# Prompt attention head by head and value pages in column strips, threaded through the gate units of a hybrid decoder step

## The chip, the cores and the metric
The kernel runs on one core of a Trainium2 chip. The metric is the device time of one launch in microseconds (us), the median of several runs. A profiled execution has a time of its own, and its span runs from the first to the last instruction on the core. Engines: TensorE (PE, with its weight loads listed as PEld), VectorE (DVE), ScalarE (ACT), GpSimd (POOL), SyncE (SP). Each works off its own queue in order and waits on semaphores.

## The reference, cut to what matters
One layer for a prompt of 256 tokens and 8 samples of one token each (together 264 columns), all float32, width 2048:

```python
h = rms_norm(x, norm1_w);  z = h @ w_in        # conv B,C,X | q,k,v | memory q | 3 gates of 2048
y_conv = (zb * short_conv(zc * zx)) @ w_conv_out
o  = (softmax(q1 k1^T) - lam * softmax(q2 k2^T)) V    # 8 heads, head width 64 + 64, values 128
y_diff = (rms_norm(o, subln_w) * (1 - lam_init)) @ w_diff_out
y_mem  = softmax(qm mk^T) mv @ w_cross_out            # 4 heads of 256 over 256 memory tokens
merged = g0 * y_conv + g1 * y_diff + g2 * y_mem       # g = sigmoid of the gate part of z
x = x + merged @ w_o;  x = x + peer_ffn(rms_norm(x))  # product-key experts, top 16 of 8 heads
```

For the prompt, keys, values and memory come from this step. Each sample has 16 pages of 128 cached keys and values, found through a page table, and 256 cached memory tokens.

## The kernel before, in words
Every engine has its own program, written out by hand in the order in which the work is to run; there is no planner. The stages follow each other on PE:

- Lines 541 to 598: norms, transposes and the projections for q, k, v, memory q and the convolution, while DVE and POOL work through the samples' key pages.
- Lines 625 to 635: keys and values of the prompt's memory; the convolution's state; own scores of the samples.
- Lines 637 to 670: a gate unit (`gate_chunk`) is 16 matmuls of 128x264 into bank 0 or 1 (one gate chunk), then 8 matmuls into bank 2 (one branch chunk). ACT takes the sigmoid, DVE multiplies and adds (a merge). There are 48 units: 16 for the convolution branch, 16 for memory, 16 for differential attention. Before the gate matmuls a unit waits for the sigmoid two units back (`gate_done`), before the branch matmuls for the merge of the unit ahead of it (`y_taken`). The first 8 units (`PART`) carry small steps of the samples' softmax at given places.
- Lines 680 to 726: prompt attention as a stage of its own, two heads at a time in two halves of PSUM. ACT copies queries, keys and values to a work area, PE turns them, ACT copies them out, PE makes the scores, DVE adds the mask and takes maxima, ACT the exponentials, DVE normalises, PE turns the weights back, ACT copies, PE multiplies with the values, ACT copies the outputs.
- Lines 734 to 780: units 8 to 15, each with one sample's values. Two memory pages and ten value pages are multiplied on PE with the weights of 4 or 8 heads as the stationary operand (line 752: two matmuls of 512 columns a page), six pages are weighed and summed on DVE (`weigh_page`) and go through PE as one more. The sums for all heads by all columns are masked to each head's own columns on DVE (`mask_sums`) and turned to a column by eight small matmuls (`columns`, line 761). POOL fetches pages into a ring of 4 slots for PE and 2 for DVE (line 459).
- Lines 782 to 800: units 16 to 47, with the sums of the sub-norm after unit 23.
- From line 802: output projection, router projection, and the expert stage, which gathers rows of two large tables.

SP streams the weights of gates and branches through a ring of two blocks (lines 284 to 320); a block serves two units. The memory key norm on DVE (line 1400) comes between the merges of units 4 and 5.

Of the kernel before, what the change touches and what calls it, by code (L numbers as in the profile page):

```python
# [19 lines left out]
ds = bass.ds  # L20
# [55 lines left out]
def build(nc, A, O):  # L76
# [16 lines left out]
    with ctx:  # L93
# [3 lines left out]
        def sem(name):  # L97
# [24 lines left out]
        PART = 8  # L122
        temp = [ring4[:, :, :].rearrange("p a b -> p (a b)"), bregion[:, :]]
# [12 lines left out]
        mask = work[:, 0:2 * TP].rearrange("p (t n) -> p t n", t=2)  # L136
        sg = work[:, 1024:1024 + 2 * NT].rearrange("p (s n) -> p s n", s=2)
# [35 lines left out]
        weighed = work[:, 0:DC]  # L173

        own_heads = [sq_mkv[0:n, o:o + DC] for n, o in ((MH, 2 * DC), (HEADS, 3 * DC))]
# [16 lines left out]
        a_now = [zst[:, n, 0:PAGES * HEADS].rearrange("p (t h) -> p t h", t=PAGES) for n in range(2)]  # L192
        am_now = [zst[:, n, PAGES * HEADS:PAGES * HEADS + 2 * MH].rearrange("p (t h) -> p t h", t=2) for n in range(2)]
        Ad_f, Sm_f = cs_rows, Sm[:, :, :, :].rearrange("p a b c -> p (a b c)")
        tmpm = small[:, 0:3, :].rearrange("p a b -> p (a b)")[:, 0:NT]
# [5 lines left out]
            exp_in exp_out sum_in sum_full a_ready attn_staged tt_full qk_T s_full sm_ready exp_ready  # L201
# [5 lines left out]
            n2_in lam_pre lam_exp x1_rows n2_ss sums_free weights_staged dpage_used weighed_ready  # L207
            weighed_used sums_masked columns_done sub_taken gather_turn loop_turn""".split()
# [4 lines left out]
        v_landed = [sem(f"v_landed{i}") for i in range(VR + DR)]  # L213
# [39 lines left out]
        selfA = small[:, 4, 64:128].rearrange("p (h b) -> p h b", h=HEADS)  # L253

# [4 lines left out]
        def _(sp):  # L259
# [32 lines left out]
            for b in range(3):  # L292
                if b == 0:
                    for r in range(NR):
                        sp.wait_ge(s["chunk_full"], C_O - 2 * (NR - 1 - r))
                        fetch(r, w_in, gate_col[b] + r * BLK)

                    sp.wait_ge(s["chunk_full"], C_O)
                    for r in range(NR):
                        branch_weights(b, r, r)  # L300
                    for n in (2, 3):
                        gate_weights(b, n, n % NR)
                        branch_weights(b, n, n % NR)
                    for n in (4, 5):
                        gate_weights(b, n, n % NR)

                    sp.wait_ge(s["attn_done"], 2)
                    for n in (4, 5):
                        branch_weights(b, n, n % NR)
                    for n in (6, 7):  # L310
                        gate_weights(b, n, n % NR)
                        branch_weights(b, n, n % NR)
                else:
                    for r in range(NR):
                        gate_weights(b, r, r)
                        branch_weights(b, r, r)
                    with sp.Fori(0, 8 // NR - 1) as i:
                        for r in range(NR):
                            gate_weights(b, NR + r, r, i)
                            branch_weights(b, NR + r, r, i)  # L320
# [14 lines left out]
        def _(pool):  # L335
# [3 lines left out]
            pool.sem_inc(s["vpage_used"], VR)  # L339
            pool.sem_inc(s["dpage_used"], DR)  # L340
# [88 lines left out]

            pool.wait_ge(s["a_ready"], 1)  # L430
            st(nc.gpsimd.memset(mask[:, :, :], 0.0))
# [4 lines left out]
            pool.wait_ge(s["mk_ready"], 1)  # L436
            for c, name in ((0, "mem_k_prompt"), (1, "mem_v_prompt")):
                pool.dma_start(O[name][0, 0].rearrange("(t p) h d -> p t (h d)", p=P),
                               mkv[:, :, c * DC:(c + 1) * DC]).then_inc(s["mkv_stored"], 16)


            pool.wait_ge(s["attn_done"], 2)
            pool.wait_ge(s["qk_stored"], 64)
            with pool.Fori(0, TS) as b:
                for k in range(DP):

                    for n in (2 * k, 2 * k + 1, PV + k):
                        if n < PV:
                            pool.wait_ge(s["vpage_used"], b * PV + (n + 1))
                            r = n % VR  # L450
                        else:
                            pool.wait_ge(s["dpage_used"], b * DP + (k + 1))
                            r = VR + k % DR
                        if n < 2:
                            src = cmem_v[ds(b * NM + n * P, P), :]
                        else:
                            page = pool.value_load(pt[0:1, ds(b * PAGES + (n - 2), 1)], min_val=0, max_val=POOL_PAGES - 1)
                            src = cache_v[ds(page * PAGE, PAGE), :]
                        pool.dma_start(v_slots[r], src).then_inc(v_landed[r], 16)  # L459


            pool.wait_ge(s["vpage_used"], TS * PV + VR)
            pool.wait_ge(s["dpage_used"], TS * DP + DR)
            pool.dma_start(x_rows[:, 0:2, :], A["x_prompt"][0].rearrange("(t p) d -> p t d", p=P)).then_inc(s["x_again"], 16)
            pool.dma_start(x_rows[0:TS, 2, :], A["x_sample"].rearrange("b t d -> (b t) d")).then_inc(s["x_again"], 16)
# [69 lines left out]
        def _(pe):  # L535
# [64 lines left out]
            def conv_state():  # L600
                pe.wait_ge(s["conv_ready"], 1)
                pe.wait_ge(s["rows_taken"], 32 + 2)
                for j in range(BC):
                    last = nc.tensor.transpose(ps[0:2 + TS, 4 + j // 4, (j % 4) * P:(j % 4 + 1) * P], conv[:, BC + j, TP - 2:NT], ident[:, :])
                last.then_inc(s["cs_full"], 1)

            def own_scores():

                pe.wait_ge(s["self_in"], 1)
                mm(ps[:, 7, 0:P], ones[0:TS, :], small[0:TS, 0, :], start=True, stop=True).then_inc(s["self_full"], 1)  # L610

            def turn_maxima(m, n):
                pe.wait_ge(s["max_full"], m + 1)
                nc.tensor.transpose(ps[0:n, 5, 0:P], small[:, 1, 0:n], ident[:, :]).then_inc(s["max_diag"], 1)

            def spread_maxima(m, n):
                pe.wait_ge(s["mb_full"], m + 1)
                mm(ps[:, 6, 0:n], ones[0:n, :], small[0:n, 2, 0:n], start=True, stop=True).then_inc(s["max_diag"], 1)

            def sum_partitions(m, n):  # L620
                pe.wait_ge(s["sum_in"], m + 1)
                mm(ps[:, 7, 0:n], ones[:, :], small[:, 1, 0:n], start=True, stop=True).then_inc(s["sum_full"], 1)
# [10 lines left out]
            conv_state()  # L633
            own_scores()
            pe.wait_ge(s["chunk_taken"], C_O + 4)

            def gate_chunk(b, r, c, q, operand, between=None, ready=None):

                pe.wait_ge(s["gate_done"], q + 1)
                for k in range(KC):  # L640
# [3 lines left out]
                    if between:  # L644
                        between(k)
# [4 lines left out]
                for k in range(BC):  # L650
# [3 lines left out]
                    if between:  # L654
                        between(KC + k)
# [3 lines left out]
            after = {(0, KC - 1): (turn_maxima, 0, nk), (0, KC + BC - 1): (spread_maxima, 0, nk), (1, KC + BC - 1): (sum_partitions, 0, nk),  # L659
                     (2, KC + BC - 1): (turn_maxima, 1, nm), (3, KC - 1): (spread_maxima, 1, nm), (4, KC - 1): (sum_partitions, 1, nm)}  # L660
            for q in range(PART):
                g, r, c = q // 2, q // 2 % NR, q % 2
# [3 lines left out]

                def softmax_step(k):
                    if (q, k) in after:
                        after[q, k][0](*after[q, k][1:])
                gate_chunk(0, r, c, q, conv[:, 0:BC, :], softmax_step)  # L670
            pe.wait_ge(s["a_ready"], 1)
            pe.wait_ge(s["gate_done"], PART + 2)
            pe.wait_ge(s["y_taken"], PART + 2)


            def flat(u):
                b = 4 - 4 * u
                return ps[:, b:b + 4, :].rearrange("p a b -> p (a b)")

            def attention(n_heads, base, w):  # L680
                halves = w // P
                a0 = 1536
                s0 = 512 * halves
                with pe.Fori(0, n_heads // 2) as i:
                    for u in range(2):
                        pe.wait_ge(s["attn_staged"], i * 2 + (base + u + 1))
                        for o in range(2):
                            for f in range(halves):
                                for t in range(2):
                                    last = nc.tensor.transpose(  # L690
                                        flat(u)[:, (o * halves + f) * 256 + t * P:(o * halves + f) * 256 + (t + 1) * P],
                                        temp[u][:, (2 * o + t) * w + f * P:(2 * o + t) * w + (f + 1) * P], ident[:, :])
                        last.then_inc(s["tt_full"], 1)
                    for u in range(2):
# [1093 lines left out]
```

## Time and profile before
| what | value |
|---|---|
| median of 3 runs (lowest, highest) | 3098.11 us (3096.09, 3110.02) |
| the profiled execution, its span | 3102.36 us, 3100.2 us |
| mean granted clock of TensorE in it | 0.945 |
| busy: PE, DVE, ACT, POOL | 2669.5, 1488.6, 370.3, 1047.9 us |

A busy time says how long an engine had an instruction in work, not that it was at its peak; ends of matmuls are modelled, so two neighbours can overlap in the records by a short tail. The granted clock is a share of 2.4 GHz. A float32 matmul shows as two instructions, each with its weight load.

### The profile page before, as it was taken

The numbers are of one execution on the slowest core, as the hardware profiler recorded it, in microseconds if no ns is written. First come the engines' busy times: TensorE is split into PE (matmuls) and PEld (weight loads), VectorE is DVE, ScalarE is ACT, GpSimd is POOL, SyncE is SP. The second block draws the span as 40 slices with busy tenths as digits, with TensorE's granted clock in tenths as the row PEclk, the third lists the DMA queues.
The fourth block names the chain that finished last, engine by engine and source line by source line (L and its number), as shares of the span: only waits on it lengthen the run. The fifth ranks groups of instructions, "written<-read, shape, count | busy, mean of one in ns | idle before, by whom it ended". The sixth has DMA issues, their size and how long they took to land.

```text
span 3100.2 us, 29862 instructions
## 1 busy us (share of the span) xinstructions
PE 2669.5 (86%) x9145; PEld 1635.6 (53%) x9145; DVE 1488.6 (48%) x2527; ACT 370.3 (12%) x816; POOL 1047.9 (34%) x952
## 2 busy tenths in 40 slices
PE   6899999895699999999999968777789959777777
PEld 4678888774433336888887743333233314233333
DVE  1456567733233331120002768887655455555543
ACT  3111000013400000100002111101111101111110
POOL 1256562200022220000000555556644545555532
PEclk9899999997799999999998989999989979999999
DMA  5599996931177875353443999999999999999999
GB/s 159 182 314 329 324 334 235 329 121 68 36 248 267 269 260 192 125 174 126 135 135 109 355 359 419 421 417 413 413 421 419 416 365 422 418 421 416 415 421 380
DMA packets 305386, 913.54 MB, mean 295 GB/s; under 512 B 15634, under 2 KB 195946, under 8 KB 236652
## 3 DMA queue, kind: packets, MB, share of 16 engines
q0 software_dynamic: 122304, 723.48, 58.8%
q1 hardware_dynamic: 182980, 188.92, 18.8%
q8 instruction: 38, 0.62, 0.1%
q14 instruction: 64, 0.52, 0.0%
HBM read 905.80 MB, written 6.56 MB: 294 GB/s over the span
## 4 chain that ended last, share of the span: by engine, by line
PE 58%; DMA 21%; DVE 10%; issue 5%; POOL 5%; ACT 1%; ACTq 0%; DVEq 0%; POOLq 0%; SPq 0%
PE ps L564 19%; PE ps L641 11%; DMA sb_S<-in_peer_u_dram,sb_ring 8%; PE ps L844 6%; PE ps L752 6%; PE ps L651 6%; DMA sb_bregion<-in_peer_u_dram,sb_ring 5%; PE ps L631 3%; DVE sb_bregion L1688 2%; DVE sb_S L1688 1%; POOL sb_bregion L478 1%; DMA sb_S<-in_peer_v_dram,sb_ring 1%; DMA sb_wring<-in_peer_v_dram,sb_ring 1%; DMA sb_wring<-in_w_in_dram 1%; DMA sb_mkv<-in_peer_u_dram,sb_ring 1%
## 5 line engine op out<-in xcount | busy, mean ns | idle before, releaser
L844 PE MATMUL ps<-sb_wring,sb_ring 128*128 128x512 f32 x992 | 468.8, 624 | 132.6 <-DMA sb_wring<-in_peer_v_dram,sb_ring 80.4
L564 PE MATMUL ps<-sb_hT,sb_wring 128*128 128x264 f32 x2304 | 534.7, 394 | 16.0 <-DMA sb_wring<-in_w_peer_q_dram 7.1
L564 PEld LDWEIGHTS ps<-sb_hT,sb_wring 128*128 128x128 f32 x2304 | 443.5, 194 | 99.3 <-issue 19.8
L844 PEld LDWEIGHTS ps<-sb_wring,sb_ring 128*128 128x128 f32 x992 | 191.2, 199 | 411.4 <-issue 282.0
L1688 DVE CUSTOM_DVE_ANT_0 sb_bregion<-sb_bregion,sb_rows 128x2048 f32<-128x2048 f32 x128 | 293.8, 2295 | 228.7 <-DMA sb_bregion<-in_peer_u_dram,sb_ring 221.0
L641 PE MATMUL ps<-sb_hT,sb_wring 128*128 128x264 f32 x1536 | 375.3, 396 | 18.5 <-DMA sb_bregion<-in_w_conv_out_dram 18.5
L641 PEld LDWEIGHTS ps<-sb_hT,sb_wring 128*128 128x128 f32 x1536 | 288.1, 192 | 122.1 <-issue 76.3
L478 POOL DMA_INDIRECT sb_bregion<-in_peer_u_dram,sb_ring x132 | 192.0, 1454 | 271.3 <-DVEq L1140 210.3
L844 PE MATMUL ps<-sb_hT,sb_ring 128*128 128x512 f32 x496 | 232.4, 618 | 44.4 <-DMA sb_hT<-in_peer_v_dram,sb_ring 34.3
L844 PE MATMUL ps<-sb_oreg,sb_ring 128*128 128x512 f32 x496 | 226.0, 603 | 39.9 <-DMA sb_oreg<-in_peer_v_dram,sb_ring 34.6
L1107 ACT ACTIVATE sb_ring<-sb_ident,sb_ring 128x128 f32<-128x128 f32 x248 | 99.7, 402 | 913.8 <-PE ps L844 705.4
L1688 DVE CUSTOM_DVE_ANT_0 sb_S<-sb_S,sb_rows 128x2048 f32<-128x2048 f32 x64 | 146.7, 2293 | 109.4 <-DMA sb_S<-in_peer_u_dram,sb_ring 105.6
L1688 DVE CUSTOM_DVE_ANT_0 sb_mkv<-sb_mkv,sb_rows 128x2048 f32<-128x2048 f32 x64 | 146.7, 2293 | 106.2 <-DMA sb_mkv<-in_peer_u_dram,sb_ring 103.2
L478 POOL DMA_INDIRECT sb_wring<-in_peer_v_dram,sb_ring x128 | 160.7, 1255 | 95.0 <-PE ps L844 53.6
L844 PEld LDWEIGHTS ps<-sb_hT,sb_ring 128*128 128x128 f32 x496 | 95.0, 197 | 179.9 <-issue 138.6
L752 PE MATMUL ps<-sb_rows,sb_zst 128*8 128x512 f32 (+1 forms) x384 | 185.7, 607 | 1.8 <-DMA sb_rows<-in_cache_mem_v_dram 1.8
L844 PEld LDWEIGHTS ps<-sb_oreg,sb_ring 128*128 128x128 f32 x496 | 92.4, 192 | 170.2 <-issue 144.3
L1517 DVE SCALAR_TENSOR_TENSOR sb_S<-sb_rows,sb_zst,sb_S 128x128 f32<-128x128 f32 x320 | 87.6, 347 | 155.0 <-DMA sb_rows<-in_cache_v_dram 154.7
L1551 DVE TENSOR_TENSOR sb_small<-sb_S,ps 128x264 f32<-128x264 f32 x32 | 13.7, 429 | 289.5 <-PE ps L651 289.2
L459 POOL DMA_DIRECT2D sb_rows<-in_cache_v_dram x128 | 68.0, 531 | 235.3 <-issue 231.3
L478 POOL DMA_INDIRECT sb_mkv<-in_peer_u_dram,sb_ring x66 | 102.5, 1553 | 128.3 <-DVEq L1140 105.3
L510 POOL COPY sb_ring<-sb_ring 128x16 int32<-128x16 int32 x16 | 18.3, 1141 | 371.4 <-DVEq L1140 371.4
(349 smaller groups left out, 2861.8 us busy)
## 6 DMA issues: line engine op xcount, KB each, us to landing
sb_wring<-in_w_in_dram SPq DMA_DIRECT2D x52, 2048.0 KB, 11.4
sb_rows<-in_cache_v_dram POOLq DMA_DIRECT2D x128, 512.0 KB, 4.8
sb_ring<-in_cache_k_dram POOLq DMA_DIRECT2D x64, 512.0 KB, 6.6
sb_mkv<-in_cache_k_dram POOLq DMA_DIRECT2D x64, 512.0 KB, 6.1
sb_wring<-in_w_mem_kv_dram SPq DMA_DIRECT2D x8, 2048.0 KB, 8.7
sb_wring<-in_w_o_dram SPq DMA_DIRECT2D x8, 2048.0 KB, 8.1
sb_wring<-in_w_peer_q_dram SPq DMA_DIRECT2D x8, 2048.0 KB, 12.4
sb_ring<-in_cache_mem_k_dram POOLq DMA_DIRECT2D x16, 512.0 KB, 6.8
```

Source lines behind the costliest of these rows:

```text
L459: pool.dma_start(v_slots[r], src).then_inc(v_landed[r], 16)
L478: nc.gpsimd.indirect_dma_start(dst, None, table, bass.IndirectOffsetOnAxis(ap=idx, axis=0)).then_inc(landed, 16)
L510: st(nc.gpsimd.tensor_copy(uidx[:, g % 4, :], idx_flat[:, g * TOPK:(g + 1) * TOPK]))
L564: last = mm(ps[:, (2 * r + c) % 4, 0:NT], wring[:, r, k, c * P:(c + 1) * P], rhs[:, k, :], start=(k == 0), stop=(k == KC - 1))
L631: last = mm(ps[:, 2 * r + t, 0:BLK], memT[:, k, t * P:(t + 1) * P], wring[:, r, k, :], start=(k == 0), stop=(k == KC - 1))
L641: last = mm(ps[:, c, 0:NT], wring[:, r, k, c * P:(c + 1) * P], hT[:, k, :], start=(k == 0), stop=(k == KC - 1))
L651: last = mm(ps[:, 2, 0:NT], bwring[:, r, k, c * P:(c + 1) * P], operand[:, k, :], start=(k == 0), stop=(k == BC - 1))
L752: last = mm(ps[0:w.shape[1], bank + q, :], w, block[:, q * 512:(q + 1) * 512], start=first, stop=final)
L844: last = mm(ps[:, 4 * t + q, :], diag[:, k % 4, :], e_slots[v % ER][:, q * 512:(q + 1) * 512], start=False, stop=q_stop, skip_group_check= ...
L1107: st(A_(diag[:, k % 4, :], ident[:, :], ACT.Copy, scale=wexp[:, g % 4, j:j + 1]))
L1517: st.run(STT(weighed[:, at], page, w, weighed[:, at], ALU.mult, ALU.add))
L1688: st(V.tensor_tensor_reduce(out=u_slots[n % UR], in0=u_slots[n % UR], in1=h2, scale=1.0, scalar=0.0, op0=ALU.mult, op1=ALU.add, accum_out= ...
```

## The change
It does five things.

1. Prompt attention is no longer a stage. Its 12 heads (now the 4 memory heads first, then the 8 differential ones) run one at a time, head a in units 2a+1 and 2a+2. PE's steps sit at fixed matmuls of a unit: turning at 0 and scores at 8 of the odd unit, turning back at 6 and values at 14 of the even one (`aside`). Queries, keys and values are read where they lie, without staging; one work area and banks 3 to 5 serve all heads.
2. The samples' values go through PE entirely, no page through DVE. A round takes four pages, each into its own 32 output partitions of banks 6 and 7 (`value_round`). Four rounds hold the memory pages of all samples (units 7 to 10), 32 rounds the value pages (units 11 to 26, two a unit), four rounds a sample. Masking and columns follow per sample, or per two samples for memory: 12 times in all.
3. Pages go to 11 slots, in places that are free by then; POOL issues them in one fixed order.
4. Units 0 to 31 are written out; a merge of the later branches signals behind its second step. The sub-norm's steps sit in units 28 to 31.
5. The memory key norm is done right behind the page maxima, ahead of the samples' memory scores; ACT takes its root between memory chunks 10 and 11. The prompt's memory stores come earlier on POOL, and the state's transposes use banks 6 and 7.

```diff
@@ slots @@
-        VR, DR = 4, 2
-        v_slots = [rows[:, t, c * DC:(c + 1) * DC] for t in range(2) for c in range(3)]
-        DP = 6
-        PV = 2 + PAGES - DP
+        late_slots = [sq_mkv[:, n * DC:(n + 1) * DC] for n in range(4)]
+        early_slots = [rows[:, 2, n * DC:(n + 1) * DC] for n in (0, 1, 3, 2)] + [ring_flat[:, D + DC:2 * D], work[:, 0:DC], work[:, DC:2 * DC]]
+        v_slots = late_slots + early_slots
+        MEM_PAGES, VPAGES = 2 * TS, (2 + PAGES) * TS
+        MEM_ROUNDS = MEM_PAGES // 4
+        QUAD = 32
@@ POOL @@
+            def load_page(p):
+                slot = page_slot(p)
+                earlier = [e for e in range(p) if page_slot(e) == slot]
+                if earlier:
+                    pool.wait_ge(s["vpage_used"], earlier[-1] + 1)
...
+                pool.dma_start(v_slots[slot], src).then_inc(v_landed[slot], 16)
@@ PE @@
+            def value_round(n):
+                pages = range(4 * n, 4 * n + 4)
+                if n == 0:
+                    pe.wait_ge(s["a_ready"], 1)
+                elif n < MEM_ROUNDS:
+                    pe.wait_ge(s["sums_masked"], n)
+                elif n % 4 == 0:
+                    pe.wait_ge(s["sums_masked"], MEM_ROUNDS + (n - MEM_ROUNDS) // 4)
+                for p in pages:
+                    pe.wait_ge(v_landed[page_slot(p)], 16 * (page_use(p) + 1))
+                for q in range(2):
+                    for p in pages:
+                        g = p % 4
...
+                        last = mm(ps[g * QUAD:g * QUAD + w.shape[1], 6 + q, :], w, v_slots[page_slot(p)][:, q * 512:(q + 1) * 512], start=first, stop=final)
+                        if q == 1:
+                            last.then_inc(s["vpage_used"], 1)
+            def aside(q, k):
...
+                a = (q - 1) // 2
+                if 0 <= a < ATTN:
+                    if (q % 2, k) == (1, 0):
+                        turn_in(a)
+                    if (q % 2, k) == (1, 8):
+                        scores_of(a)
+                    if (q % 2, k) == (0, 6):
+                        turn_back(a)
+                    if (q % 2, k) == (0, 14):
+                        outputs_of(a)
+                if 7 <= q < 11 and k == 18:
+                    value_round(q - 7)
+                if 8 <= q < 12 and k == 10:
+                    columns(q, q - 8)
+                if 11 <= q < 27 and k in (6, 18):
+                    value_round(MEM_ROUNDS + 2 * (q - 11) + k // 18)
+                if 13 <= q < 29 and q % 2 and k == 12:
+                    columns(q, MEM_ROUNDS + (q - 13) // 2)
...
+            for q in range(32):
...
+                if q == 6:
+                    pe.wait_ge(s["columns_kept"], 1)
+                if 9 <= q < 13:
+                    pe.wait_ge(s["columns_kept"], q - 7)
+                if 14 <= q < 30 and q % 2 == 0:
+                    pe.wait_ge(s["columns_kept"], 1 + MEM_ROUNDS + (q - 12) // 2)
+                gate_chunk(b, r, c, q, oT_mem if b else conv[:, 0:BC, :], aside, "vo_ready" if b else None)
@@ ACT, one unit @@
+            for q in range(32):
+                a = (q - 1) // 2
+                inside = 0 <= a < ATTN
+                if inside and q % 2 == 1:
+                    keep_turned(a)
+                if q == 1:
+                    sample_exponentials()
+                if inside and q % 2 == 0:
+                    keep_weights(a)
+                sigmoid(q)
+                if inside and q % 2 == 1:
+                    exponentials(a)
...
+                if inside and q % 2 == 0:
+                    keep_output(a)
@@ DVE, one unit @@
+            for q in range(5, 32):
+                a = (q - 1) // 2
+                if 8 <= q < 12:
+                    mask_sums(q - 8)
+                if 13 <= q < 29 and q % 2:
+                    mask_sums(MEM_ROUNDS + (q - 13) // 2)
+                if a < ATTN and q % 2:
...
+                    maxima_of(a)
+                    normalise(a)
...
+                if 13 <= q < 29 and q % 2:
+                    keep_columns(q, MEM_ROUNDS + (q - 13) // 2)
...
+                if q < 16:
+                    first_merge(q)
+                else:
+                    later_merge(q)
```

## Rows read from the trace of the kernel before

**Rows 1.** Windows by stage: us; busy PE, PEld, DVE, ACT, POOL; clock; DMA share; GB/s.

```profile
624.26:713.74 89.48, 89.48 (x394) 75.56 (x394) 27.17 (x36) 13.40 (x18) 2.81 (x5) 0.97 0.37 124
713.74:843.80 130.06, 71.10 (x274) 52.47 (x273) 44.58 (x93) 62.25 (x156) 0.00 (x0) 0.70 0.05 16
843.80:1186.86 343.06, 336.90 (x1072) 126.01 (x1072) 123.66 (x408) 11.54 (x28) 77.91 (x147) 0.97 0.77 258
1186.86:1535.20 348.34, 346.53 (x1553) 294.37 (x1552) 50.17 (x78) 23.46 (x40) 1.29 (x2) 1.00 0.46 147
1535.20:3100.20 1565.00, 1270.20 (x3356) 623.57 (x3356) 886.05 (x1570) 186.01 (x402) 714.49 (x544) 0.94 0.92 376
```

**Rows 2.** PE's timeline in plain gate units: start, length, instructions in a row.

```profile
692.36 7.28 PE L641 MATMUL ps<-sb_hT,sb_wring 128*128 128x264 f32 x32
699.48 3.72 PE L651 MATMUL ps<-sb_conv,sb_bregion 128*128 128x264 f32 x16
703.04 7.28 PE L641 MATMUL ps<-sb_hT,sb_wring 128*128 128x264 f32 x32
```

**Rows 3.** PE's timeline in a unit with values.

```profile
1021.69 1.16 PE L641 MATMUL ps<-sb_hT,sb_wring 128*128 128x264 f32 x4
1022.77 1.88 PE L752 MATMUL ps<-sb_rows,sb_zst 128*4 128x512 f32 x4
...
1024.59 1.16 PE L641 MATMUL ps<-sb_hT,sb_wring 128*128 128x264 f32 x4
```

**Rows 4.** PE's timeline: own values, and columns of one sample.

```profile
843.79 1.92 PE L731 MATMUL ps<-sb_small,sb_rows 8*128 8x8 f32 x16 [1.38 <-DVEq L1140]
...
1185.00 1.94 PE L761 MATMUL ps<-sb_ones,sb_mkv 8*128 8x1 f32 x16
```

**Rows 5.** PE's timeline in prompt attention: turning, scores, values.

```profile
716.56 0.66 PE L690 MATMUL ps<-sb_ident,sb_ring 128*128 128x128 f32 x4 [2.67 <-ACTq L1010]
...
741.27 2.08 PE L700 MATMUL ps<-sb_ring 64*128 64x256 f32 x8
743.14 1.91 PE L700 MATMUL ps<-sb_bregion 64*128 64x256 f32 x8
...
754.82 1.92 PE L720 MATMUL ps<-sb_ring 128*128 128x256 f32 x4
...
806.30 1.50 PE L690 MATMUL ps<-sb_ident,sb_ring 128*128 128x128 f32 x8 [3.06 <-ACTq L1010]
...
809.94 2.06 PE L704 MATMUL ps<-sb_ring 128*128 128x256 f32 x8
```

**Rows 6.** Windows of two of these stretches.

```profile
741.20:745.00 3.80, 3.80 (x17) 2.52 (x16) 1.57 (x2) 0.60 (x1) 0.00 (x0) 0.50 0.00 0
754.80:758.40 3.60, 3.60 (x10) 2.38 (x8) 0.00 (x0) 0.98 (x2) 0.00 (x0) 0.50 0.00 0
```

**Rows 7.** ACT's timeline: a sigmoid, exponentials of one head, a table load.

```profile
710.36 0.39 ACT L983 ACTIVATE sb_zst<-ps 128x264 f32<-128x264 f32 x1 [10.29 <-PE ps L641]
...
726.37 0.51 ACT L1020 ACTIVATE sb_bregion<-sb_bregion,sb_stat 128x256 f32<-128x256 f32 x1 [0.83 <-DVEq L1140]
...
728.26 0.19 ACT L1020 ACTIVATION_READ_ACCUMULATOR sb_bregion<-sb_bregion,sb_stat 128x1 f32 x1
...
736.58 1.28 ACT L1007 ACT_TABLE_LOAD   x1 [0.33 <-ACT sb_oreg L1031]
```

**Rows 8.** DVE's timeline: first turned maxima, memory key norm, one head's normalisation.

```profile
634.29 0.29 DVE L1334 TENSOR_REDUCE sb_stat<-ps 128x1 f32<-128x128 f32 x1 [15.99 <-PE ps L614]
...
684.86 2.29 DVE L1406 TENSOR_REDUCE sb_small<-sb_oreg 128x8 f32<-128x2048 f32 x1
...
726.43 0.18 DVE L1462 RECIPROCAL sb_stat<-sb_stat 128x4 f32<-128x4 f32 x1
...
728.21 0.48 DVE L1467 SCALAR_TENSOR_TENSOR sb_ring<-sb_ring,sb_stat 128x256 f32<-128x256 f32 x1
```

**Rows 9.** The value pages' line on POOL: issue to landing.

```profile
DMA to landing us min/median/max: 3.4/4.8/9.2
```

More of the change, by code:

```diff
@@ L190, in build @@
         small = sb("small", [P, 5, P])
[L192 to L195, printed above, removed]
+        head_rows, halves = stat[:, 48:48 + HEADS], stat[:, 56:58]
+        mask = small[:, 0:4, :].rearrange("p a b -> p (a b)").rearrange("p (t n) -> p t n", t=2)
+        Sm_f = Sm[:, :, :, :].rearrange("p a b c -> p (a b c)")
         names = """consts x_in x_clear mem_in cols_in st_in small_in lam_in rope_in pt_in x_ss x_scaled xT_full xT_taken
@@ L316, in _ @@
                         branch_weights(b, r, r)
[L317 to L320, printed above, removed]
+                with sp.Fori(0, 8 // NR - 1) as i:
+                    for r in range(NR):
+                        gate_weights(b, NR + r, r, i)
+                        branch_weights(b, NR + r, r, i)
             stream(8, w_o, 0, C_O, ("y_full", 48))
@@ new lines, in columns, with sub_sums @@
+            def columns(q, m):
+                pe.wait_ge(s["gate_done"], q + 2)
+                pe.wait_ge(s["sums_masked"], m + 1)
+                pick = halves if m < MEM_ROUNDS else ones[:, 0:1]
+                n = pick.shape[1]
+                for h in range(BC):
+                    last = mm(ps[:, (q + 1) % 2, NT + h * n:NT + (h + 1) * n], own_heads[:, h * P:(h + 1) * P], pick, start=True, stop=True)
+                last.then_inc(s["columns_done"], 1)
+            def sub_sums(h0):
+                pe.wait_ge(s["sub_in"], 1)
+                for h in range(h0, h0 + 4):
+                    if h >= 4:
+                        pe.wait_ge(s["sub_taken"], h - 3)
+                    mm(ps[:, 4 + h % 4, 0:NT], ones[:, :], sq_mkv[:, h * NT:(h + 1) * NT], start=True, stop=True).then_inc(s["sub_full"], 1)
@@ L974, in _, with sigmoid @@
             root(4, small[:, 3, 0:60])
-            with st.loop(3, 4) as i:
-                for q in range(4):
-                    memory_chunk(i, 4 + q)
-            for q in range(PART):
+            for n in range(4, 11):
+                memory_chunk(n // 4, n % 4)
+            root(5, small[:, 3, 0:8])
+            for n in range(11, 16):
+                memory_chunk(n // 4, n % 4)
+            def sigmoid(q):
                 act.wait_ge(s["gate_full"], q + 1)
@@ new lines, in exponentials @@
+            def exponentials(a):
+                u = a % 2
+                act.wait_ge(s["sm_ready"], a + 1)
+                for n in range(2 if a < MH else 4):
+                    if a < MH:
+                        dst, src, scale = temp[:, 1024 + n * 256:1024 + (n + 1) * 256], AREA[:, 1024 + n * 256:1024 + (n + 1) * 256], MD ** -0.5
+                    else:
+                        dst, scale = temp[:, 512 + n * 256:512 + (n + 1) * 256], DK ** -0.5
+                        src = dst
+                    st.run(A_(dst, src, ACT.Exp, scale=scale, bias=stat[:, 16 * u + 4 + n:16 * u + 5 + n],
+                              accum_out=stat[:, 16 * u + 8 + n:16 * u + 9 + n]))
+                st.settle()
+                act.sem_inc(s["exp_ready"], 1)
@@ new lines, in sample_exponentials, with memory_exponentials @@
+            def sample_exponentials():
+                act.wait_ge(s["exp_in"], 1)
+                st.run(A_(work, work, ACT.Exp, scale=DK ** -0.5))
+                st(A_(small[:, 0, :], small[:, 0, :], ACT.Exp, scale=DK ** -0.5))
+                act.sem_inc(s["exp_out"], 1)
+            def memory_exponentials():
+                act.wait_ge(s["exp_in"], 2)
+                st(A_(Sm_f, Sm_f, ACT.Exp, scale=MD ** -0.5))
+                act.sem_inc(s["exp_out"], 1)
+            act.wait_ge(s["token_done"], 2 + 2 * TS)
@@ L1058, in _ @@
[L1058 to L1060 removed]
+            gates_of(32, 16)
             to_stage(16, C_O, R_O)
```

646 lines of the change are left out of this document (286 added, 360 removed).

## The prediction
> **What bounds the kernel now.** I cut the span into stages with the windows view [rows 1]. The five windows are: the first eight gate units, prompt attention, the eight gate units that carry the sample values, the other 32 gate units, and all that follows. The reader is to see that TensorE (PE) is busy in four of the five, and that only prompt attention is different: 71 us of PE work in 130 us, at a mean granted clock of 0.70 and a DMA share of 0.05. There PE waits in turn for ScalarE (ACT) and VectorE (DVE), head pair by head pair. The third window is the longest for its work: 343 us for eight units, against 89.5 us for the eight ahead of it. PE is busy all through it (336.9 of 343.1 us), so its length is PE work, and transfers (258 GB/s, share 0.77) run behind it.
>
> From the first gate matmul to the end of the 48th unit is 624.26 to 1535.2, 910.9 us. Everything that the change moves lies in this stretch, apart from the memory key norm and the stores.
>
> **The change part by part.** A gate unit that carries nothing repeats every 10.68 us (703.04 less 692.36) [rows 2]. The 48 units stay: 89.5 us for the first eight with their sample softmax steps, 8 x 10.68 = 85.4 for the next eight once they carry nothing, and 348.3 for the last 32 with the sub-norm sums [rows 1]. Sum 523.2 us.
>
> Removed: the 130.1 us attention stage [rows 1] as a stage of its own, its staging copies on ACT, the ring of six weighed pages on DVE, and the value matmuls of the third window. That window is 343.1 us, of which 85.4 are its plain units.
>
> Added to PE inside the units, first attention. A memory head turns eight 128x128 blocks (1.50 us), scores with eight instructions (1.9 of the 2.06 us, without the 0.17 us tail that overlaps), turns four blocks back (0.66) and multiplies with the values (again 1.9) [rows 5]; all of it is 6.0 us. A differential head turns four (0.66), scores in eight 64-row instructions, turns four (0.66) and multiplies with four (0.9). The scores took 1.87 us at a granted clock of 0.50, the 1.2 GHz level [rows 5, 6]; inside dense units I take the other level, and half of it, 0.93, with 0.3 for switching. That is 3.5 us. 4 x 6.0 + 8 x 3.5 = 52 us. The samples' own values are the 1.92 us of today, and the columns of 12 rounds of sums 12 x 1.94 = 23.3 us, where there are 16 now [rows 4].
>
> Then the value pages, the largest term. Today four instructions on one page (two halves of 512 columns, each float32 product as two instructions) occupy 1.88 us, 1.71 without the tail, so 0.4275 us each. The cycle from one group of four gate instructions to the next is 2.90 us [rows 3]: 0.89 for those (32 in 7.12, the 7.28 of a row without its tail [rows 2]), 1.71 for the page, and 0.30 to switch there and back. The new kernel does four pages at a time, each in its own 32 output partitions: 16 instructions a round, 36 rounds (4 for memory, 32 for pages).
> No row of before shows instructions in different column strips. From above, one after the other: 16 x 0.4275 + 0.30 = 7.14 us. From below, all four strips at once: 4 x 0.4275 + 0.30 = 2.01. The nearest row is that of the 64-row scores, which use two halves of the array: eight instructions start to start in 1.87 us, 0.234 each, at the granted clock 0.50, while four full-array instructions of the same 256 columns took 1.92 - 0.21 = 1.71, 0.427 each, at the same clock [rows 5, 6]. Two halves thus run 1.8 abreast. I explain it by the order of issue: each product is two instructions in the same strip, the second can't start before the first is done, and instructions start in order; so the second of one strip runs beside the first of the next, and no more. Sixteen instructions then take nine slots: 9 x 0.4275 + 0.30 = 4.15 us. I take this: 36 x 4.15 = 149.4 us.
>
> The waits. In an odd unit with a differential head, PE may not begin the next unit before DVE has copied the columns, and DVE does that behind the head's normalisation. From the end of the gate matmuls: sigmoid 0.39, a table load 1.28, four exponentials 2.1 (726.37 to 728.45) [rows 7], normalisation 2.3 (726.43 to 728.69) [rows 8], copy 0.2 and hand-overs of some 0.8 make 7.1 us. Beside it stand eight branch matmuls (3.56 [rows 2]) and the second round (4.15), 7.7 us. So it is hidden with 0.6 us to spare. In unit 5 there is no round; its memory head has two exponentials less, and I count 1 us of stall there. The masking of sums at the start of an odd unit works on half the elements of the 2.29 us reduction [rows 8], so about 1.2 us; behind a merge it ends before the next round, which comes after seven matmuls (3.1) and a turning (0.66). I put all such stalls at 5 us.
> Page issue on POOL is hidden: eight pages a unit against about 21.6 us of unit, with 4.8 us to landing [rows 9]; and eleven slots let the next two rounds be fetched ahead. Transfers: 144 pages of 0.524 MB and ten pairs of weight blocks of 3.15 MB lie in units 7 to 26, 107 MB in some 425 us, 252 GB/s: the rate that the third window has now [rows 1].
> The memory key norm moves ahead of the samples' memory scores. From the reduction at 684.86 its end is 692.7; with the product ahead of it some 10 us of DVE, about 12 with the root. The scores, the state copy and the first maxima come so much later, but DVE sat idle for 15.99 us until the first turned maxima [rows 8]. Nothing is lost, with 4 us to spare; without the cover it would be 12 us. The prompt's stores and the memory stores move with POOL's queue, by no more than that.
>
> Sum: 523.2 + 52 + 1.9 + 23.3 + 149.4 + 5 = 754.8 us against 910.9: 156 us less. The profiled execution took 3102.4 us (span 3100.2), so 2946; the median of the runs shown is 3098.1, 4.3 us lower, so 2942 us.
>
> **The rivals.** *Four strips abreast.* If the two instructions of a product don't hold up the next strip, a round is 2.01 us, 77 us less in all. For it: the strips share no output partitions. Against it: the 1.8 of two halves, which pairwise order explains. The round then no longer covers the columns copy: 7.1 - 3.56 - 2.01 = 1.5 us in eight odd units, 12 us back. Time 2942 - 77 + 12 = 2877 us. Transfers would stand at 5.8 MB in some 18 us, 320 GB/s, close to what share 0.77 for 258 GB/s leaves (335).
> The Trainium skill, "TensorE: Matmul & The Clock Gate", section "Part 3: Packing small matmuls — row/col tiling", gives 2.38 times for three column strips and 3.07 for four row strips; by it a round would be some 2.5 us, an estimate, and the time near 2890 us. By the same section instructions start and end in order, which agrees with the 1.8 above [rows 5].
>
> *No overlap.* A strip may be an output address and no more. Then a round is 7.14 us, 108 us more: 3050. For it: no row shows column strips overlapping. Against it: two row halves do.
>
> *Slower: each change of strip drains the array.* If an instruction in another strip must await the end of the one before, tail included, a round costs 16 x (0.4275 + 0.17) + 0.30 = 9.9 us, 5.7 more than forecast, 36 x 5.7 = 206 us: 3148, slower than now. It decides from 8.5 us a round (4.15 + 156 / 36). For it: the 0.30 us that PE loses today at each page's coming and going [rows 3]. Against it: the two halves of the scores don't drain.
> On this the Trainium skill, "TensorEngine Tiling (Array Packing)", section "Key Properties", says that a change of tiling mode drains TensorE but a change of tile within a mode doesn't; the 0.30 us agrees with the first half, and the second speaks against this rival.
>
> *The feed is late.* Page transfers, weights and POOL's in-order queue share the sixteen units with pages; at 220 GB/s a unit is 26 us instead of 21.6, 16 x 4.6 = 74 us more: 3016. Against it: the third window moved 258 GB/s [rows 1], and PE is busy in it all but 6.2 us.
>
> **How the numbers follow.** Forecast 0.60; four abreast 0.12; no overlap 0.13; late feed 0.10; drain 0.05. The range 2875 to 3055 takes in both bounds of a round and the late feed. What a measurement of this kernel can tell from no change is about 0.5%, 15 us. Faster by more than that: the first four cases less a little for several mishaps together, 0.91; within it 0.04; slower 0.05.
>
> **What would show it.** Right: 48 units in 755 us; odd units near 22 us with two rounds; rounds of about 4.1 us on PE; granted clock near 1.00 from 624 us on; no PE wait for pages above some microseconds; what follows the gates unchanged at 1565 us. Wrong: rounds of 7 us or 2 us (size of the main term), gaps at the starts of even units (columns copied late), or PE waiting for page landings.

## The result, and the profile after

The changed kernel takes 2865.45 us, the median of 4 runs (2863.17 to 2866.91), against 3097.1 us (3095.34 to 3110.02) for the kernel before: a ratio of 0.924, 95% interval 0.922 to 0.927. It is faster, by more than forecast, and 10 us below the low end of the range.

The windows view of the changed kernel, with the columns of [rows 1]: all 48 gate units, and what follows them.

```profile
629.01:1299.20 670.19, 661.11 (x3386) 509.23 (x3386) 133.54 (x241) 102.51 (x197) 83.66 (x157) 1.00 0.66 230
1299.20:2864.70 1565.50, 1273.81 (x3357) 624.55 (x3356) 886.14 (x1570) 185.82 (x402) 716.26 (x544) 0.93 0.92 376
```

The reader is to see that the 910.9 us of four windows before have become 670.2, at a mean granted clock of 1.00 (0.50 in the first 3 us), and that the rest is as long as it was (1565.0 before). So all of the gain lies in the stretch that the prediction took apart; it had 754.8 there. The stretch begins at 629.01 us instead of 624.26, so that 4.8 us are lost ahead of it.

PE's timeline in two units of the changed kernel, as in [rows 2 and 3]: scores of a differential head (L697), columns (L759), a round of four pages that lie in one tile (L748), and the start of the next unit.

```profile
794.96 1.16 PE L650 MATMUL ps<-sb_hT,sb_wring 128*128 128x264 f32 x4
796.05 1.13 PE L697 MATMUL ps<-sb_ring 64*128 64x256 f32 x8
797.12 1.16 PE L650 MATMUL ps<-sb_hT,sb_wring 128*128 128x264 f32 x4
798.11 1.84 PE L759 MATMUL ps<-sb_stat,sb_ring 128*128 128x2 f32 x16
799.81 2.47 PE L650 MATMUL ps<-sb_hT,sb_wring 128*128 128x264 f32 x10
802.12 1.50 PE L660 MATMUL ps<-sb_conv,sb_bregion 128*128 128x264 f32 x6
803.55 1.91 PE L748 MATMUL ps<-sb_rows,sb_Ad 128*8 128x512 f32 x16
805.38 2.49 PE L660 MATMUL ps<-sb_conv,sb_bregion 128*128 128x264 f32 x10
808.91 3.35 PE L650 MATMUL ps<-sb_hT,sb_wring 128*128 128x264 f32 x14 [1.03 <-DVEq L1179]
```

Sixteen value instructions take 1.91 us, tail included (the modelled end of the last one, 0.17 us). Four took 1.88 before [rows 3]. The next round has its pages in two tiles, so that the view lists them apart, and the starts can be read:

```profile
820.86 0.61 PE L748 MATMUL ps<-sb_mkv,sb_Ad 128*8 128x512 f32 x3
820.88 0.60 PE L748 MATMUL ps<-sb_rows,sb_Ad 128*8 128x512 f32 x1
821.29 0.61 PE L748 MATMUL ps<-sb_mkv,sb_Ad 128*8 128x512 f32 x3
821.31 0.59 PE L748 MATMUL ps<-sb_rows,sb_Ad 128*8 128x512 f32 x1
```

Four instructions, one of each page, start within 0.02 us, and the next four 0.43 us later. Four strips run abreast. Below, a slot is these 0.43 us, the time from one instruction of a strip to the next.

The last row of the first block is the wait that the prediction looked for at the starts of even units. DVE's timeline shows what PE waits for there: the copy of the columns (L1534) stands behind the head's normalisation (L1501 to L1508).

```profile
806.26 0.18 DVE L1501 RECIPROCAL sb_stat<-sb_stat 128x4 f32<-128x4 f32 x1 [6.34 <-ACTq L1040]
...
807.39 0.88 DVE L1508 SCALAR_TENSOR_TENSOR sb_ring<-sb_ring,sb_stat 128x256 f32<-128x256 f32 x2
808.42 0.18 DVE L1534 COPY sb_oreg<-ps 128x16 f32<-128x16 f32 x1
```

In the list of PE's waits from 622 to 1310 us (waited for: us in total, times, longest) there are nine such waits, and none for a page:

```profile
PE ps L650 <- DVEq L1179: 9.1, 9, 1.0
```

### The profile page after: what moved, and what is told of

Read it like the earlier page. It is cut to its first block, busy times and chain, and to the rows that moved or that the text cites. A ratio compares the mean times of both kernels' runs of the same rounds, so it can differ in the third digit from the quotient of the medians.

```text
span 2864.7 us, 28284 instructions
## 1 busy us (share of the span) xinstructions
PE 2489.0 (87%) x9241; PEld 1596.7 (56%) x9241; DVE 1383.8 (48%) x2157; ACT 360.9 (13%) x771; POOL 1050.5 (37%) x952
## 4 chain that ended last, share of the span: by engine, by line
PE 53%; DMA 23%; DVE 9%; issue 6%; POOL 6%; ACT 2%; DVEq 0%; POOLq 0%; SPq 0%; ACTq 0%
PE ps L573 20%; PE ps L650 12%; DMA sb_S<-in_peer_u_dram,sb_ring 8%; PE ps L660 5%; DMA sb_bregion<-in_peer_u_dram,sb_ring 5%; PE ps L877 5%; PE ps L640 3%; DMA sb_mkv<-in_peer_u_dram,sb_ring 3%; DMA sb_wring<-in_w_in_dram 2%; DMA sb_wring<-in_peer_v_dram,sb_ring 2%; PE ps L748 2%; POOL sb_bregion L487 2%; DVE sb_bregion L1746 2%; DMA sb_S<-in_peer_v_dram,sb_ring 1%; POOL sb_wring L487 1%
## 5 line engine op out<-in xcount | busy, mean ns | idle before, releaser
L519 POOL COPY sb_ring<-sb_ring 128x16 int32<-128x16 int32 x16 | 16.6, 1040 | 345.7 <-DVEq L1179 345.6
L660 PE MATMUL ps<-sb_oreg,sb_bregion 128*128 128x264 f32 x512 | 122.1, 388 | 0.0
L573 PE MATMUL ps<-sb_conv,sb_wring 128*128 128x264 f32 x512 | 116.3, 387 | 1.9 <-DVEq L1179 1.8
L640 PE MATMUL ps<-sb_wring,sb_bregion 128*128 128x256 f32 x512 | 110.7, 379 | 0.0
L660 PEld LDWEIGHTS ps<-sb_oreg,sb_bregion 128*128 128x128 f32 x512 | 96.4, 190 | 25.4 <-issue 9.4
```

The costliest lines, as they stand in the source:

```text
L519: st(nc.gpsimd.tensor_copy(uidx[:, g % 4, :], idx_flat[:, g * TOPK:(g + 1) * TOPK]))
L573: last = mm(ps[:, (2 * r + c) % 4, 0:NT], wring[:, r, k, c * P:(c + 1) * P], rhs[:, k, :], start=(k == 0), stop=(k == KC - 1))
L640: last = mm(ps[:, 2 * r + t, 0:BLK], memT[:, k, t * P:(t + 1) * P], wring[:, r, k, :], start=(k == 0), stop=(k == KC - 1))
L660: last = mm(ps[:, 2, 0:NT], bwring[:, r, k, c * P:(c + 1) * P], operand[:, k, :], start=(k == 0), stop=(k == BC - 1))
```

## The experiments

Each kernel is the changed one with one edit, but for the last two. A round is sixteen instructions, four to a page; in the first two experiments the start and stop marks of the sums follow the strips. Times are set beside the changed kernel's 2865.45 us; the ratios are to the kernel before.

**One strip for all four pages.**

```diff
-                        g = p % 4
+                        g = 0
```

> All four pages of a round write the same 32 output partitions, so that their products stand in one line; the waits, transfers and counts stay (the samples' memory values come out mixed up). If the gain of the change comes from strips that run abreast (theory: all four at once), a round goes back from about 1.9 us to 16 x 0.4275 = 6.84 us and more, 36 x 5.0 = 180 us, less some 8 us of stalls that the longer rounds cover: about 3037 us (3020 to 3055), with rounds of 6.8 to 7.0 us on PE. By the theory of the prediction (pairs by order of issue, nine slots) the step is 7 slots, 36 x 3.0 = 108 us: 2973 us. If the strips have nothing to do with the gain: 2865 us.

Measured 3042.1 us (3038.75 to 3044.91), ratio 0.982 (0.979 to 0.985): 177 us of the 232 gained are gone. PE's timeline shows one round:

```profile
813.39 7.03 PE L748 MATMUL ps<-sb_mkv,sb_Ad 128*8 128x512 f32 x16
820.35 1.16 PE L650 MATMUL ps<-sb_hT,sb_wring 128*128 128x264 f32 x4
```

Sixteen instructions in line take 7.03 us, 16 x 0.43 and a tail. The strips are three quarters of the gain, at the size that four abreast gives; pairs (2973) are out. The other 55 us, attention inside the units less the value work that PE took over from DVE, have no experiment of their own.

**Two strips.**

```diff
-                        g = p % 4
+                        g = p % 2
```

> The four pages of a round share two strips, alternating. If strips run fully abreast, whatever the order of issue, a round is 16 / 2 = 8 slots, 3.42 us instead of 1.9: 36 x 1.55 = 56 us more, less up to 8 us of stalls covered: 2915 us (2905 to 2925). By pairs in order of issue it is nine slots, as it would be with four strips: 2865 us, no change. (The samples' memory values come out mixed up.)

Measured 2916.6 us (2914.52 to 2930.98), ratio 0.942 (0.938 to 0.946). A round:

```profile
809.33 3.61 PE L748 MATMUL ps<-sb_rows,sb_Ad 128*8 128x512 f32 x16
812.87 2.49 PE L660 MATMUL ps<-sb_conv,sb_bregion 128*128 128x264 f32 x10
```

3.61 us, eight slots and a tail. So a round lasts as long as its fullest strip: 4, 8 or 16 instructions of 0.43 us with four, two or one strip. By the prediction's nine slots this kernel would have been no slower than the changed one.

**Pages outside, halves inside.** The program then issues both products of a page ahead of the next page's.

```diff
-                for q in range(2):
-                    for p in pages:
+                for p in pages:
+                    for q in range(2):
```

> The two loops of a round change places: both halves of a page first, then the next page. The four products of neighbours in the program then go to one strip in turn. If each strip takes its own instructions whatever the order in the program, a round stays at 4 slots: 2865 us, within 0.5%. If instructions start strictly in the program's order and one that waits for its strip holds back all behind it, a round is 13 slots, 5.56 us: 36 x 3.7 = 133 us more, less 8 of stalls: about 2990 us. Something between would mean a short look-ahead.

Measured 2862.47 us (2860.47 to 2866.11), ratio 0.923 (0.921 to 0.926): no change. A round of it in PE's timeline, again with pages in two tiles:

```profile
818.93 0.62 PE L748 MATMUL ps<-sb_mkv,sb_Ad 128*8 128x512 f32 x3
818.97 0.60 PE L748 MATMUL ps<-sb_rows,sb_Ad 128*8 128x512 f32 x1
819.36 0.62 PE L748 MATMUL ps<-sb_mkv,sb_Ad 128*8 128x512 f32 x3
819.40 0.59 PE L748 MATMUL ps<-sb_rows,sb_Ad 128*8 128x512 f32 x1
...
820.78 2.49 PE L660 MATMUL ps<-sb_conv,sb_bregion 128*128 128x264 f32 x10
```

The last page's first instruction starts 0.04 us after the first page's, though twelve instructions of the other pages stand before it in the program. A strip that is busy doesn't hold up what is issued behind it for another strip. That an engine works off its queue in order, as the opening says, is not so for PE's starts where the strips differ.

**No rounds at all.** The matmuls of the rounds are left out, and with them the samples' page values; waits and counts stay.

```diff
-                        last = mm(ps[g * QUAD:g * QUAD + w.shape[1], 6 + q, :], w, v_slots[page_slot(p)][:, q * 512:(q + 1) * 512], start=first, stop=final)
                         if q == 1:
-                            last.then_inc(s["vpage_used"], 1)
+                            pe.sem_inc(s["vpage_used"], 1)
```

> The matmuls of the 36 value rounds are left out; their waits and counts stay (the samples' page values are zero). Theory of four abreast: a round is 1.71 to 2.0 us, so 62 to 72 us less; but a round no longer covers the copy of the columns at the ends of odd units, which gives back up to 8 x 1.9 = 15 us: 2808 us (2793 to 2825). If a round were the 4.15 us forecast, 149 us less: about 2730. If pages can't be fed in units so short (107 MB in some 340 us, 315 GB/s), PE waits for landings and the gain is smaller than 50 us.

Measured 2821.6 us (2819.08 to 2823.34), 44 us less, near the upper end of the times expected. What hid the rest is in PE's waits and in its timeline behind one of them:

```profile
PE ps L650 <- DVEq L1178: 25.3, 9, 3.1
```

```profile
828.12 5.04 PE L650 MATMUL ps<-sb_hT,sb_wring 128*128 128x264 f32 x14 [3.05 <-DVEq L1178]
```

The nine waits grew from 9.1 to 25.3 us, since no round covers the columns' copy any more. And the 14 gate instructions behind a 3.05 us wait take 5.04 us in place of the 3.35 behind one of 1.03: the windows view gives a granted clock of 0.66 for 828.10 to 833.10 here, and 1.00 for 808.90 to 812.30 in the changed kernel. Eight of the nine waits are of 3.05 us or a little more, and the gate instructions behind these eight take 14.5 us more in all than 3.35 each. From the first gate matmul to the first of the output projection this kernel takes 630.6 us (622.90 to 1253.54) against 672.0 (629.01 to 1301.05), 41.4 less. 41.4 + 16.2 + 14.5 = 72 us for 36 rounds, 2.0 each.

**The key norm behind the memory scores again**, its root behind the projection copies on ACT.

```diff
-            memory_key_norm()
             with st.loop(TS // 2, 8) as i:
...
+            memory_key_norm()
```

> The memory key norm goes back behind the samples' memory scores, its root behind the sixteen projection copies; nothing else moves. Theory: ahead of the scores it holds up the memory key pages, these then compete with the first gate weights, and the first gate unit starts late. The first gate matmul starts at about 624 us, as in the kernel before, where the five profiles with the norm ahead have 622.9 to 629.8 (mean 626.9): about 3 us less, 2862 us, within what can be told from no change. Rival: the order costs nothing and the start only varies from run to run: 2865 us, with a start anywhere in 623 to 630.

This kernel and the next three ran on one chip. Measured 2857.5 us (2857.05 to 2859.88), ratio 0.922 (0.920 to 0.925); the kernel with eight slots, which behaves as the changed one, had 2865.78 (2860.79 to 2868.34) there. 8 us less, more than the 3 expected, and no overlap of the runs. First the changed kernel's windows around the end of the memory projection, then this one's; with each its first gate matmul and, from the view of transfers, its first block of branch weights (the last number is the time from issue to landing):

```profile
570.00:580.00 10.00, 10.00 (x48) 8.79 (x48) 8.25 (x7) 0.98 (x3) 0.00 (x0) 1.00 0.26 73
...
620.00:630.00 10.00, 0.99 (x2) 0.84 (x3) 8.64 (x8) 0.00 (x0) 0.22 (x1) 0.50 1.04 405
...
629.01 6.19 PE L650 MATMUL ps<-sb_hT,sb_wring 128*128 128x264 f32 x20 [23.00 <-issue]
...
sb_bregion<-in_w_conv_out_dram SPq DMA_DIRECT2D x1, 1024.0 KB, 23.7
```

```profile
570.00:580.00 10.00, 10.00 (x48) 8.79 (x48) 6.54 (x7) 0.38 (x1) 2.12 (x4) 1.00 0.86 303
...
620.00:630.00 10.00, 7.36 (x26) 6.08 (x27) 6.47 (x13) 0.00 (x0) 4.21 (x8) 0.71 0.60 201
...
622.64 8.95 PE L650 MATMUL ps<-sb_hT,sb_wring 128*128 128x264 f32 x32 [14.89 <-issue]
...
sb_bregion<-in_w_conv_out_dram SPq DMA_DIRECT2D x1, 1024.0 KB, 15.6
```

With the norm ahead, the transfers stand at a share of 0.26 while DVE norms and POOL asks for no memory key page, and at 1.04 from 620 to 630, where the first weights should be there already. POOL asks for the last memory key page some 16 us later (616.42 for 600.54), and behind it for the prompt's stores (617.74 for 601.86). The first branch block, which the first unit waits for, is asked for at 605.18 us and takes 23.7 to land; with the old order it is asked for at 606.92 and takes 15.6. In both kernels the first gate matmul starts 0.1 us after that landing. The first gate matmul came at 622.9 to 629.8 in the seven profiles with that order (mean 627.4), and at 622.6 and 620.7 in the two with the old one (624.3 in the kernel before, which has it too). So the start is worth about 5 us on the mean, 6.4 between these two profiles; the rest of the 8 us has no row of its own. From the first gate matmul to the first of the output projection both take 672 us (629.01 to 1301.05, 622.64 to 1294.8).

**The columns' copy ahead of the normalisation** on DVE.

```diff
                     maxima_of(a)
-                    normalise(a)
...
                     keep_columns(q, MEM_ROUNDS + (q - 13) // 2)
+                if a < ATTN and q % 2:
+                    normalise(a)
```

> On DVE the copy of the columns (and of the own values in unit 5) goes ahead of the head's normalisation; nothing else moves. Theory: the nine waits of 0.86 to 1.03 us at the starts of even units are this copy alone, so PE's 9.1 us of waits for DVE go and nothing takes their place: 2856 us. Rival: behind the copy the normalisation or the merge is late next, and half or more of the 9.1 us comes back at the turning back or at the branch matmuls: 2861 us or more.

Measured 2854.97 us (2853.72 to 2856.53), ratio 0.921 (0.919 to 0.923), 10.8 us less than the kernel with eight slots. Its waits from 622 to 1310 and the copy on DVE:

```profile
PE ps L650 <- issue: 25.5, 1, 25.5
PE ps L573 <- DVEq L1179: 1.8, 1, 1.8
```

```profile
798.69 0.17 DVE L1534 COPY sb_oreg<-ps 128x16 f32<-128x16 f32 x1
804.89 0.18 DVE L1501 RECIPROCAL sb_stat<-sb_stat 128x4 f32<-128x4 f32 x1 [6.03 <-ACTq L1040]
```

The copy now lies in DVE's idle time before the exponentials; the nine waits are gone and none came in their place.

**Eight page slots in place of eleven.**

```diff
-            return 4 + p % 7 if p < MEM_PAGES else (p - MEM_PAGES) % 11
+            return 4 + p % 7 if p < MEM_PAGES else (p - MEM_PAGES) % 8
```

> The sample pages go through eight slots in place of eleven, so that one round is fetched ahead instead of nearly two. Theory (the feed is hidden, as forecast): a slot is free some 8 us before its next page is due twice over, 3.4 to 9.2 us to landing fit in, 2865 us, with no PE wait for a landing above a microsecond. Rival (the shorter rounds make the feed tight, some 320 GB/s in the units with pages): PE waits for landings at L735 rows or at rounds, 10 to 40 us more: 2875 to 2905.

Measured 2865.78 us (2860.79 to 2868.34), ratio 0.925 (0.922 to 0.927): no change. PE's only wait for pages:

```profile
PE ps L748 <- DMA sb_mkv<-in_cache_v_dram: 0.9, 3, 0.3
```

The feed is hidden even one round ahead, at the 312 GB/s and a share of 0.87 that the changed kernel shows from 735 to 1065. The three extra slots bought nothing.

**Both edits**, the norm back and the copy ahead.

> Both edits together: norm behind the scores, copies of columns ahead of the normalisation. By the theories of the two 3 + 9 us less, 2853 us; by their rivals 2861 to 2865.

Measured 2849.17 us (2845.11 to 2852.79), ratio 0.920 (0.918 to 0.922): 16.6 us less than with eight slots on the same chip; the two gains, 8.3 and 10.8, nearly add (19.1).

**Both edits, and later stores of the prompt**, behind the memory stores; the diff shows the stores. On DVE the state copy and the samples' first maxima also go ahead of the key norm.

```diff
-                pool.dma_start(O[po][0, 0].rearrange("(t p) h d -> p t (h d)", p=P),
-                               rows[:, 0:2, c * DC:(c + 1) * DC]).then_inc(s["qk_stored"], 16)
...
+            for c, po in ((1, "k_prompt"), (2, "v_prompt")):
+                pool.dma_start(O[po][0, 0].rearrange("(t p) h d -> p t (h d)", p=P),
+                               rows[:, 0:2, c * DC:(c + 1) * DC]).then_inc(s["qk_stored"], 16)
```

> On top of both edits, the stores of the prompt's keys and values (2 x 1.05 MB) go behind the state copy and the memory stores, so that they no longer share the transfers with the first gate and branch weights; the state copy and the samples' first maxima go ahead of the norm on DVE, so that they are not late for an earlier unit. Theory (transfers set the start of the first gate unit): 2.1 MB at some 380 GB/s is 5.5 us, the first gate matmul moves from 620.7 to about 615.5, less what PE then waits for the first maxima: 2844 us (2841 to 2847). Rival (the start is set by the order in which the weight blocks are asked for, or by DVE): start within 2 us of 620.7, 2849 us.

Measured 2840.64 us (2839.07 to 2850.01), ratio 0.917 (0.916 to 0.919): the fastest version, 25 us under the changed kernel, though on another chip than the other experiments (the kernel before took 3100.62 us there and 3098.58 where the both-edits kernel ran). That is better than the 2844 expected, but the profile tells only part of why. It was taken of the slowest execution, 2850.01 us, and there the first gate matmul starts only 1.5 us earlier:

```profile
619.25 9.79 PE L651 MATMUL ps<-sb_hT,sb_wring 128*128 128x264 f32 x32 [9.95 <-issue]
```

In that execution PE also ended the memory projection later, at 609.3 us, and SP asks for the first branch block only at 608.47, where in the profile of both edits it asks at 604.63. The block then takes 10.7 us to land, 16.0 there:

```profile
sb_bregion<-in_w_conv_out_dram SPq DMA_DIRECT2D x1, 1024.0 KB, 10.7
```

So 5.3 us of landing are gone, near the 5.5 expected, and 3.8 of them went by the later asking in this execution. From the first matmul of the output projection on, which no edit touches, it took 1567.4 us, and 1560.5 to 1563.8 in the other nine profiles of the changed kernel and its variants, so a few us between two profiles can come from there. Whether the stores' absence from this stretch is the whole gain stays open.

## Why the prediction was wrong

Its stages and its list of terms held; one term was twice too long. The stretch term by term, from the rows above:

| term | forecast, us | measured, us |
|---|---|---|
| 48 units | 523.2 | 523.2, taken over (a plain unit is again 10.68) |
| attention | 52 | 43.5: 4 x 4.78 + 8 x 3.05 |
| own values | 1.9 | 1.9 |
| columns | 12 x 1.94 = 23.3 | 12 x 1.80 = 21.6 |
| value rounds | 36 x 4.15 = 149.4 | 36 x 2.03 = 73.1 |
| waits at even units | 5 | 9.1 |
| sum | 754.8 | 672.4 (the window has 670.2, which leaves 521.0 for the units) |

A round is 1.83 us from its first instruction to the next matmul (803.55 to 805.38), and 0.10 before it: the first of six instructions of 0.2225 us starts at 802.12, so they end at 803.45. Another 0.10 is in the branch matmuls behind it: ten take 2.49 us, where ten of 0.2225 and a tail would be 2.39. That makes 2.03, four slots and 0.3 for coming and going, as in the sum of the rival.

**The step that failed** is the sentence on the order of issue: "the second of one strip runs beside the first of the next, and no more", and from it nine slots. It rested on 1.8 abreast for the 64-row scores [rows 5, 6]. But those use two halves of the array. With two halves 2.0 is all there is: full overlap would be four slots of 0.427, 1.71 us. The length of the row couldn't tell a limit of two from full overlap. But the trace of before speaks against the order of issue in the starts, which I didn't read. Narrow windows on the line of these scores show how many of its instructions are in work (first number in brackets):

```profile
741.27:741.29 0.02, 0.02 (x2) 0.02 (x2) 0.50 0.00 0
741.87:741.88 0.01, 0.01 (x4) 0.01 (x2) 0.50 0.00 0
```

The products alternate between the halves, two instructions each. By the order of issue the first instruction would be alone for a slot; two start at once, and two more are in work 0.6 us later. That first step is 0.16 longer than a slot, the difference between 1.87 and 1.71. In the changed kernel the same eight instructions take 1.07 us, and some 0.20 are lost before and behind them, against 0.85 for four slots of 0.213. The edit of two strips and the edit of the order both speak against pairs. I named four abreast as a rival, at 0.12 and 2877 us; its size of a round, 2.01, was right: four abreast ran in place of the nine slots, 2.03 us a round where 4.15 was forecast.

The Trainium skill, "TensorE: Matmul & The Clock Gate", section "Part 3: Packing small matmuls — row/col tiling", also has a model of the span: the length of one matmul and some 4 ns for each further tile. The rows come near that, with four starts within 0.02 us; its 2.38 times for three strips, which I cited, doesn't carry over to four strips here, where 7.03 us became 1.91, 3.7 times. That matmuls start strictly in order, as the section says, is not what the rows of the edited order show, nor the windows above, although the prediction read its 1.8 as agreeing with it.

**Attention** was forecast with rows of the old stage. For the differential heads' scores I halved the row because of the clock of 0.50 [rows 6]; the turnings I took with their tails, and the memory heads' rows at the clock that they had (0.68 from 806.30 to 807.90 us, where the turning of 1.50 us lies). The changed kernel's timeline has a memory head's turning and scores inside a unit:

```profile
642.04 0.60 PE L684 MATMUL ps<-sb_ident,sb_rows 128*128 128x128 f32 x4
642.48 0.60 PE L684 MATMUL ps<-sb_ident,sb_mkv 128*128 128x128 f32 x4
642.92 3.73 PE L650 MATMUL ps<-sb_hT,sb_wring 128*128 128x264 f32 x16
646.48 1.89 PE L693 MATMUL ps<-sb_ring 128*128 128x256 f32 x8
648.21 3.28 PE L650 MATMUL ps<-sb_hT,sb_wring 128*128 128x264 f32 x14
```

Eight turnings take 0.88 us start to start, where 1.50 was taken, the scores 1.73 where 1.9 was; in the next unit the turning back takes 0.44 (658.22 to 658.66) where 0.66 was, the values 1.73 (662.22 to 663.95) where 1.9 was: 1.2 us less a memory head, 4.9 in four. The differential heads are 0.45 less, 3.6 in eight; nearly all of that is the tails of two turnings, which stood at a clock of 1.00 already (716.50 to 717.30).

**The waits.** Their place was right, and who makes them. The round that should cover the copy was half as long, and DVE was some 0.8 us earlier than thought (copy done 6.3 us after the sigmoid began, 802.32 to 808.60), so eight waits of 1.03 us and one of 0.86 came, in place of 5 us.

**The key norm.** "Nothing is lost, with 4 us to spare" looked at DVE alone, and there it held: the first maxima are done at 632.7 us, and PE first turns them at 637.71. What was lost, about 5 us, went by the transfers: the norm holds up the memory key pages and the stores behind them, and these then run against the first weights, of which the first branch block takes 23.7 us to land instead of 15.6. In the kernel before PE waits for the same block, which lands at 624.0; PE starts at 624.26. I had counted the queue that the step is moved past, but not the transfers that start when it is done.

**What held:** the remainder of 1565 us, the clock of 1.00 (from 632 us on, after 0.50 in the first 3 us; before, it was 0.50 in the first 5), the hidden feed (320 GB/s was estimated for rounds this short, 312 measured), and no drain between strips.

The range ended at 2875 because I took the rival's time as the low end as it stood. The attention term was no firmer than the rounds; its 8.5 us would have put the low end at 2866.5, 1 us above the result.

## What to carry to other kernels

The length of a row of two things side by side can't tell a limit of two from no limit; read the starts inside it, and when a forecast needs four, take both bounds as equals and the price between them as open. Take the tail off every row and convert it to the clock that the work will run at, not only the one that looks odd. Where a step is moved past transfers, follow the transfers that it releases, and where a copy frees a bank for the next matmul, put it ahead of work that waits for another engine.

## What the runs showed of the hardware

Float32 matmuls with 128 rows and 8 output rows in four strips of 32 ran 3.7 times as fast as in one strip (7.03 to 1.91 us for sixteen instructions), in both orders of issue that ran. To come from full-width matmuls and to go back costs 0.3 us a round, as it did for one page before [rows 3]. A wait of 1.03 us left the granted clock at 1.00; after one of 3.05 us it was 0.66 over the next 5 us, which made the wait cost 1.7 us more than its length.
